# Norms inside their neighbouring stages, tokens in natural order, fewer fences and 1 MB expert pieces in a two-block transformer kernel

## The reference

```python
def first_block(x, ...):
    h = rmsnorm(x, norm_mix_g)
    proj = h @ w_in                        # 1024 x 7424
    # qkv_a: three dilated window attentions (dilations 1, 4, 16), 8 heads each, merged by log-sum-exp
    # q_b, k_b, v_b: dense grouped-query attention, 8 query heads on 2 key heads
    gates = sigmoid(gate_logits + b_gate)
    merged = gates[0] * (o_a @ w_proj_a) + gates[1] * (o_b @ w_proj_b)
    x = x + merged @ w_out
    h2 = rmsnorm(x, norm_ffn_g)
    x = x + moe_ffn(h2, ...)               # router, top 4 of 32 experts, 1024 -> 2 x 1024 -> 1024

def second_block(x, ...):
    for l in range(2):
        proj = rmsnorm(x, pre_g[l]) @ w_in[l]
        y_a = sgu_mixer(...) * silu(z_a)         # gated unit: a 128 x 128 product over tokens
        y_b = mla_mixer(...) * silu(z_b)         # attention over latents
        y_c = chunk_band_mixer(...) * silu(z_c)  # banded attention with a bias table
        merged = sum over 3 branches of sigmoid(gate) * (y @ w_branch)
        x = x + rmsnorm(merged @ w_out[l], post_g[l])
    return x
```

## Time and profile before

| what | value |
|---|---|
| median of three runs | 3405.22 us (3404.34 to 3406.01) |
| the profiled execution | 3412.55 us, its span 3410.7 us |
| TensorE busy (PE) | 3119.5 us, 91% |
| VectorE (DVE), ScalarE (ACT), GpSimd (POOL) busy | 923.4, 751.9, 100.5 us |
| chain that ended last | PE 83%, DMA 6%, DVE 6%, ACT 2% |
| loaded and stored | 575.16 MB, mean 169 GB/s |

### The profile page before, as it was taken

How to read it: one execution, slowest core, us unless ns; L and a number is a source line. 1 busy time by engine, 2 the same in 40 slices (tenths; PEclk the granted TensorE clock), 3 DMA queues, 4 the chain that set the end, 5 groups by cost and what they waited for, 6 DMA issues and landing times.

```text
span 3410.7 us, 36906 instructions
## 1 busy us (share of the span) xinstructions
PE 3119.5 (91%) x13348; PEld 1703.6 (50%) x13349; DVE 923.4 (27%) x2235; ACT 751.9 (22%) x1479; POOL 100.5 (3%) x120
## 2 busy tenths in 40 slices
PE   8999999968999899999899599988999898989997
PEld 4454654445585355574567245444444345444443
DVE  3441651142212222222211323214111224032212
ACT  2222641011212211112211124223111225131111
POOL 0000000000000000000000000010000000010000
PEclk9999999969999999999999798989999999989999
DMA  3221012247989999999994421111221211112221
GB/s 133 74 67 57 1 50 74 87 182 285 414 317 400 411 395 397 416 360 397 423 391 167 173 72 41 37 62 56 75 86 62 80 62 39 57 42 81 80 80 62
DMA packets 110500, 575.16 MB, mean 169 GB/s; under 512 B 13021, under 2 KB 20445, under 8 KB 84672
## 3 DMA queue, kind: packets, MB, share of 16 engines
q1 hardware_dynamic: 100896, 556.76, 42.6%
q0 software_dynamic: 9504, 17.07, 1.3%
HBM read 570.37 MB, written 20.97 MB: 173 GB/s over the span
## 4 chain that ended last, share of the span: by engine, by line
PE 83%; DMA 6%; DVE 6%; ACT 2%; issue 1%; DVEq 1%; ACTq 0%; SPq 0%; POOL 0%; POOLq 0%
PE banks L318 41%; PE banks L1211 12%; PE banks L1189 8%; PE banks L315 6%; PE banks L1164 6%; DMA arena<-in_w_experts 5%; PE banks L600 3%; PE banks L623 2%; PE banks L611 2%; DVE arena L673 1%; PE banks L264 1%; ACT arena L274 1%; DVE arena L685 1%; PE banks L1143 1%; DVE arena L1351 1%
## 5 line engine op out<-in xcount | busy, mean ns | idle before, releaser
L318 PE MATMUL banks<-arena 128*128 128x512 f32 (+3 forms) x3328 | 1419.4, 588 | 36.5 <-DVEq L200 28.1
L318 PEld LDWEIGHTS banks<-arena 128*128 128x128 f32 x3328 | 634.0, 192 | 795.0 <-issue 763.7
L1211 PEld LDWEIGHTS banks<-arena 128*128 128x128 f32 x3584 | 403.3, 193 | 14.5 <-issue 14.5
L1211 PE MATMUL banks<-arena 128*128 128x128 f32 x3584 | 405.0, 276 | 4.7 <-issue 4.7
L1189 PE MATMUL banks<-arena 128*64 128x512 f32 (+1 forms) x1024 | 322.6, 593 | 0.0
L1164 PE MATMUL banks<-arena 128*64 128x512 f32 x1152 | 272.7, 624 | 38.4 <-DMA arena<-in_w_experts 35.8
L315 PE MATMUL banks<-arena 128*128 128x512 f32 x512 | 220.9, 592 | 1.8 <-DVEq L200 1.8
L1189 PEld LDWEIGHTS banks<-arena 128*64 128x64 f32 (+1 forms) x1024 | 123.4, 159 | 176.2 <-issue 176.2
L1284 DVE TENSOR_TENSOR arena<-banks,arena 128x512 f32<-128x512 f32 x64 | 44.3, 692 | 564.1 <-PE banks L1211 321.1
L1164 PEld LDWEIGHTS banks<-arena 128*64 128x64 f32 x1152 | 86.1, 143 | 207.9 <-issue 206.7
L827 DVE TENSOR_TENSOR arena<-banks,arena 128x512 f32<-128x512 f32 x64 | 44.3, 693 | 512.6 <-PE banks L318 512.6
(11 more groups left out here) (208 smaller groups left out, 1822.8 us busy)
## 6 DMA issues: line engine op xcount, KB each, us to landing
arena<-in_w_experts SPq DMA_DIRECT2D x192, 2048.0 KB, 17.8
arena<-in_w_in SPq DMA_DIRECT2D x84, 1024.0 KB, 5.0
arena<-in_w_out SPq DMA_DIRECT2D x12, 1024.0 KB, 5.0
arena<-in_w_branch SPq DMA_DIRECT2D x24, 512.0 KB, 3.6
arena<-expert_rows SPq DMA_DIRECT2D x4, 2048.0 KB, 14.4
arena<-in_w_in SPq DMA_DIRECT2D x4, 832.0 KB, 4.4
arena<-in_gate_b SPq DMA_DIRECT2D x2, 1536.0 KB, 6.2
arena<-in_x SPq DMA_DIRECT2D x4, 512.0 KB, 5.2
```

What stands on the lines that cost most here:

```text
L318: last = PE.matmul(PS[:, tt, 0:ncols], lhsT(kk, tt), Wh[h][:, q, 0:ncols], start=(kk == 0), stop=(kk == kt - 1))
L1211: last = PE.matmul(PS[:, q, f * P:(f + 1) * P], ch[q][:, k, f * P:(f + 1) * P], xT[:, k], start=(k == 0), stop=(k == 7))
```

## The change

- **Norms.** `norm_stage` gives way to a class `Norm` with methods for one tile. `norm_mix` runs as an unfenced stage; `norm_ffn` runs inside `out_stage`, `norm_pre` inside `combine_stage` and inside `out_post_stage` of layer 0. Where the next product begins, PE turns tile by tile ahead of each tile of its first half of K (`turn_ahead`, through a new callable `early`).
- **Order.** x is loaded in residue order by the DMA from an unpermuted input for the first norm, then loaded again in natural order (`x_nat`). The attentions' outputs are written in natural order, POOL reorders `hT` during the dilated attention (`turn_order`), and everything from the output product on is in natural order. The output goes out per tile.
- **Merged turn.** The first half is turned inside the merge's second half, the second half ahead of the tiles of the output product; ACT copies all.
- **Fences.** `norm_mix`, `heads_1`, the output products, `gating`, `latents` and `raised` lose theirs; `raised` loads its weights early and gets its own semaphores; waits (`sgu_seen`, `tr_free`) stand in.
- **Chunk attention.** The bias tiles of the first two head pairs are made during `heads_2`; the gate multiply is split in four.
- **Experts.** Twelve pieces of 1 MB instead of six of 2 MB: each half of gate and up is cut in two by K, and the full-block path accumulates in that order. Ten pieces of expert 0 are loaded after the output product, ahead of the write of the normed rows.

```diff
@@ class Norm
+            def scale(self, dve, c, tt):
+                if tt == 0:
+                    dve.wait_ge(SEM["grow_in"], 16 * c.of("grow") + 16)
+                dve.wait_ge(SEM["norm_sd"], up(c.of("norm_sd") + tt + 1))
+                sd = self.sd[:, tt:tt + 1]
+                V.reciprocal(sd, sd)
+                V.drain()
+                V.scalar_tensor_tensor(self.hb(c)[:, tt], x3[:, tt], sd, v(GROW, D), ALU.mult, ALU.mult).then_inc(SEM["norm_h"], 1)
...
+            def turn_ahead(self, pe, c):
+
+                def early(tt):
+                    if tt == 0:
+                        self.turn(pe, c, 0)
+                    if tt + 1 < TT:
+                        self.turn(pe, c, tt + 1)
+                    pe.wait_ge(SEM["tr_free"], up(c.of("tr") + 2 * tt + 2))
+                return early
@@ heads_1, dilated
+                sp.wait_ge(SEM["norm_h"], up(4))
+                sp.dma_start(x3, A["x"][0].rearrange("(t p) d -> p t d", p=P)).then_inc(SEM["x_nat"], 16)
...
+            def turn_order(pool, c):
+
+                for k in range(0, 8, 2):
+                    for q in range(2):
+                        G.tensor_copy(v(GROW + S * q, S).rearrange("p (u r) -> p r u", r=4),
+                                      hT[:, k + q].rearrange("p (r u) -> p r u", r=4))
+                    G.drain()
+                    G.tensor_copy(hT[:, k:k + 2], v2(GROW, 2, S))
+                    G.drain()
@@ merge_stage, out_products
+            def turn(pe, c0, n, tt):
+                pe.wait_ge(SEM["applied"], up(c0.inside(n, KC).of("sig") + 4 * (nbr - 1) + tt + 1))
+                tr_pe(pe, c0, 4 * n + tt, [merged_3[:, tt, (4 * n + a) * P:(4 * n + a + 1) * P] for a in range(4)])
...
-                        dense_pe(pe, c, 2 * b, lambda kk, tt: yT[b][:, kk, tt * P:(tt + 1) * P], 4, 512)
+                        dense_pe(pe, c, 2 * b, lambda kk, tt: yT[b][:, kk, tt * P:(tt + 1) * P], 4, 512,
+                                 (lambda tt: turn(pe, c0, 0, tt)) if n and not b else None)
...
+                    dense_pe(pe, c0.inside(n, {"T": 1}), 0, lambda kk, tt: mT[:, kk, tt * P:(tt + 1) * P], 8, 512,
+                             None if n else copied, early=None if n else lambda tt: turn_last(pe, c0, tt))
@@ out_stage
+                sp.wait_ge(SEM["mm"], up(unit(c, 1, TT - 1)))
+                for q in range(2, 12):
+                    sp.dma_start(v(BIG + CH * q, CH), A["w_experts"][0, q]).then_inc(SEM[f"ch{q}"], 16)
+                sp.wait_ge(SEM["norm_h"], up(c.of("norm_h") + 4))
+                sp.dma_start(H2D.rearrange("(t p) d -> p t d", p=P), norm_ffn.hb(c)).then_inc(SEM["h2_out"], 16)
...
+                        if n and tt:
+                            norm_ffn.mean(dve, c0, tt - 1)
+                            norm_ffn.scale(dve, c0, tt - 1)
@@ expert_stage
+                    for q in range(12):
+                        sp.wait_ge(SEM["ch_free"], up(12 * j + q + 1))
+                        apart(sp, 12 * j + q + 1)
+                        sp.dma_start(v(BIG + CH * q, CH), A["w_experts"][bass.ds(e, 1), q].rearrange("o p n -> p (o n)")).then_inc(SEM[f"ch{q}"], 16)
...
+                        for h in range(2):
+                            for kh in range(2):
+                                arrived(part(2 * h, 4 * kh))
+                                arrived(part(2 * h + 1, 4 * kh))
+                                if h and kh:
+                                    turn_products(0)
+                                products(h, range(4 * kh, 4 * kh + 4)).then_inc(SEM["ch_free"], 2)
@@ combine_stage
+                    last.then_inc(SEM["x_done"], 1)
+                    if tt:
+                        norm_pre.mean(dve, c, tt - 1)
+                        norm_pre.scale(dve, c, tt - 1)
@@ latents, raised
+                pe.wait_ge(SEM["sgu_seen"], up(c.of("layer") + 1))
...
+                        if n:
+                            pe.wait_ge(SEM["raised_ev"], up(raised_unit(layer, n - 1, tt)))
+                        else:
+                            pe.wait_ge(SEM["ev"], up(unit(c, -1, tt)))
+                            pe.wait_ge(SEM["tr_free"], up(c.of("tr") - 3 + tt))
@@ chunk_stages
-                V.tensor_tensor(v(YC, 2048), v(YC, 2048), v(SC, 2048), ALU.mult)
-            heads = Stage({"T": 4}, sp=sp_, pe=pe_, act=act_, dve=dve_, lead=lead)
+                for q in range(4):
+                    dve.wait_ge(SEM["ev"], up(unit(c, 3, q)))
+                    V.tensor_tensor(v(YC + 512 * q, 512), v(YC + 512 * q, 512), v(SC + 512 * q, 512), ALU.mult)
+            heads = Stage({"T": 4}, sp=sp_, pe=pe_, act=act_, dve=dve_, lead=lead, pool=lambda pool, c: biases(pool, c, (0, 1)))
@@ out_post_stage, ACT
+                        if n:
+                            root(tt)
+                            if tt and more:
+                                norm_pre.square(act, c, tt - 1)
+                                norm_pre.root(act, c, tt - 1)
+                if more:
+                    norm_pre.copy(act, c, 0)
+                    norm_pre.square(act, c, TT - 1)
+                    norm_pre.root(act, c, TT - 1)
+                    for tt in range(1, TT):
+                        norm_pre.copy(act, c, tt)
@@ output_stage
+                for tt in range(TT):
+                    sp.wait_ge(SEM["x_done"], up(8 + tt + 1))
+                    sp.dma_start(out[0, tt * P:(tt + 1) * P], x3[:, tt]).then_inc(SEM["x_out"], 16)
```

464 lines of the change are left out of this document (246 added, 218 removed).

## The result

The changed kernel takes 3312.85 us (median of four runs, 3308.66 to 3317.64) against 3404.78 (3404.18 to 3406.01): a ratio of 0.973 (95% interval 0.971 to 0.975), 91.9 us less. Forecast were 3315 us and -90.3. A second set of five runs of the same kernel gave 3314.17 (3309.81 to 3316.71).

What follows compares the result with a forecast made beforehand. PE, busy 91% of the span, bounds the kernel, so only its waits and slow clock can yield time; terms sum to -90.3 us, execution 3322.3, median 3315 us, range 3296 to 3338.

Steps and rivals of the forecast that it cites:

- Merged turn: Three seams between merge and output product: fences and bunched transposes go, 7.6 us each, -22.9 us in all.
- Gated unit to latents, raised: Two seams, twice each: PE no longer waits for DVE's tail (-20.3 us); raised projections start earlier (-10.4 us).
- Combine, layer seam, output: Combine and norm go tile by tile (-11.6 us), likewise the layer seam (-6.0); output leaves per tile (-2.8).
- Chunk attention: Twice: scores start 1.6 us earlier and DVE's first top stops waiting for POOL, 5.8 us; -14.8 us in all.
- Experts: 1 MB weight pieces: earlier-freed buffers against slower short rows, taken as 0, with ends -18 and +22 us.
- Loss: ... 2% slower: Experts' weight queue: rows cut from 16 KB to 8 KB make transfers 2% slower, by a line through two packet sizes.
- fine pieces win: Rival in the experts: waits fall to about 35 us, giving 3297 us; chance 0.17.
- The walk through the blocks: All 32 expert blocks traced with a first-in first-out queue: -9 us with no rate loss, +3 at 2%.
- slower than before: Rival in the experts: 1 MB pieces don't overlap their fixed part, 62 us an expert, 4150 us; chance 0.03.
- POOL in the dilated attention: POOL's reordering of `hT` stays hidden in the 86 us stage, its overlap inside DVE's idle time; cost 0.
- POOL's instructions block DVE whole: Rival in the dilated attention: 12 POOL instructions of up to 3.5 us hold DVE, +10 us, 3325; chance 0.05.
- Norm and router: Seam behind the first output product: norm per tile, bound by a DVE and ACT chain, saves only 1.0 us.

Runs made afterwards that it cites:

- e4: Changed kernel with one fence put back ahead of the latents' products, twice in the run: median 3333.87 us.
- f1: Changed kernel with four repairs: earlier first turns, POOL's copies tied to scores, combine loads reordered, ACT's tile 0 copy earlier at the layer seam: 3309.31 us.
- e6: Changed kernel with the first two head pairs' bias tiles made inside chunk attention again and the gate multiply in one instruction: 3326.20 us.
- e2: Changed kernel with experts' weights waited for and freed by 2 MB again, each piece sent as two 1 MB transfers with 8 KB rows: 3320.45 us.
- f2: f1 plus idle matmuls that nobody reads in three PE pauses (ahead of the router, layer seam, combine): 3301.00 us.
- f3: f1 with all combine rows loaded ahead of the next weights, and idle matmuls ahead of the router only: 3308.77 us.
- f4: f3 with idle matmuls at the layer seam and during the combine as well: 3301.84 us.
- e7: Changed kernel with the last half of the merged tiles turned in one go ahead of the output product, no fence back: 3326.36 us.
- e1: Changed kernel with the experts' weights in six 2 MB pieces and the expert loop of before: 3317.81 us.

## Why the prediction was right, and where its terms were not

- **Merged turn.** Forecast 7.6 a seam, measured 7.7, 9.6, 7.8; most of the extra of the second is the clock of the kernel before (its merge products took 249.13 us there and 247.44 in the third). The eight turns take 0.43 us each with no pause.
- **Gated unit to latents, raised.** Forecast 15.4 a layer, measured 15.3 and 15.0; e4 measured the fence alone at 10.7, forecast 10.3 and 10.0.
- **Combine, layer seam, output.** -13.1, -5.9, -3.8 for -11.6, -6.0, -2.8. The order that sets the seam, ACT's copy of tile 0 behind its root of tile 2, is there (product at 2600.27, idle 2.69 behind ACT L280), and moving it (f1) gave 3.2 more. The forecast's "about 11 us of idle PE" for this seam does not fit its own -6.0: PE stood 13.0 us there before and 7.5 now.
- **Chunk attention.** The idle time was right (7.1 of 7.4 in e6); what I left out is the clock behind the pause, 2.9 us in e6's first layer. The whole stretch got 10.1 and 8.0 us shorter for 7.4.
- **Experts: the term that failed, inside its ends.** The step "Loss: ... 2% slower" took the slower queue to cost about as much as the finer freeing gains. The rate did fall by 2%, but in e2 that cost 0.5 us, within the spread of the stage, while the freeing gained 12 of the 25 us that I had called its most. So the rival "fine pieces win" had the mechanism and over half of its size; 0.17 was too low for it. Why the lower rate cost so little stays open: the changed kernel's queue moved over 410 GB/s in about half of the stage, which isn't little. The walk through the blocks with no loss of rate gave -9, which is nearer to the -11 than the 0 that I took.
- **The rival "slower than before".** It did not come. The price of 2.0 us plus bytes/436e3 that I quoted from the Trainium skill, "DMA: Bandwidth & Descriptors", stands there in the section "Anatomy of one DMA — SWDGE (gpsimd) path" and not in "Bandwidth", and for transfers that GpSimd issues; here SP issues them. The section "Bandwidth" asks for at least 1 MiB a transfer, which 1 MB pieces still meet. In the changed kernel an expert took 1083.5/31 = 35 us and not the 53 of that rule one transfer at a time.
- **POOL in the dilated attention.** The forecast took 0 and gave "POOL's instructions block DVE whole" a chance of 0.05. It happened: 4 to 6 us, and its sign, a DVE instruction of over 1 us (1.81), showed in the trace. The failed step took 0.62 against 0.49 us as the price of any overlap. Those 0.62 us lay wholly inside an instruction of POOL:

```profile
2295.04 0.93 POOL L1673 TENSOR_SCALAR arena<-arena 128x256 f32<-128x256 f32 x1
```

The scale began 0.06 us behind it and ended 0.25 us ahead of its end, so the reading was right for POOL's TENSOR_SCALAR. It did not carry over to POOL's COPY, which held DVE to its end; in the changed kernel both stand in one trace (a 512-wide scale of 0.62 us beside a TENSOR_SCALAR at 2962.45). Why the two differ, no run here shows. The copies were quicker than I thought (1.1 us for 512 columns, 13 us in all, not 28 to 69), which kept the loss under the rival's 10. The Trainium skill, "SBUF — State Buffer", section "SBUF: two separate sides", says that the ports which DVE and GpSimd share go for a whole instruction to whichever starts first, GpSimd's instruction or one of DVE that runs in a 2-port mode or has two inputs in SBUF. Beside POOL's copies the trace agrees in the main, with ends of both within 0.03 us, and DVE's L696 with an operand from PSUM was not held; beside POOL's TENSOR_SCALAR it does not.
- **Norm and router.** The seam itself got 2.2 us shorter, more than the 1.0; behind it the router's 64 products took 13.87 us, 10.12 before. Nine further traces with that code show 13.86 or 13.87 in eight and 11.24 in one. Before, 32 transposes ran in one go ahead of them; now PE turns in short groups between pauses, and the clock is at 0.50 when the router starts. f2 shows that it is the clock, since with PE kept busy the products took 11.35, and 10.72 and 10.83 in f3 and f4. The forecast ended this term at the router's first product.
- **Start.** I had the first product begin 0.5 us earlier; it began at 20.71, 0.1 later than before. And I left out that the turns of the last two tiles, which used to lie ahead of the product, now stand inside it at 0.87 us each: +1.9 in all.

The median came out 2 us from the forecast, and that is luck. Stage by stage the traced difference is 13 us more than forecast: experts -11.6, chunk, merge, combine and output -8.0 and latent attention -3.2 beyond it, against dilated +4.2, start +2.4 and router +3.1. The medians differ by 92 us and not by 103 because the traced execution of the kernel before lay 8 us above its median and that of the changed one 4 below. That a sum is right is no proof of its terms.

## What to carry to other kernels

Price a seam as pause plus the clock behind it: here 7.5 us of standing cost 10.7, and a shorter, choppier seam ahead of small matmuls gave its gain back. When loads run through few buffers, ask at what size a buffer comes free before asking for the best transfer; halving 2 MB pieces paid, halving again lost. Before moving copies to POOL, look at which DVE instructions work on SBUF alone meanwhile, and tie each copy to a DVE instruction that reads PSUM; take the price of an overlap only from a row with the same instruction on POOL.

## What the runs showed of the hardware beyond that

- PE's clock can fall while PE hardly stands: in f2 it was granted 1.00 over 6.2 us of wide matmuls and 0.70 over the transposes and 32-column products behind them, in which PE is busy 13.26 of 14.20 us with one pause of 0.88. The fall came in the midst of the 32-column products, while PE was busy throughout:

```profile
701.79:704.60 2.81, 2.81 (x25) 2.81 (x26) 0.00 (x0) 0.00 (x0) 0.00 (x0) 0.99 1.01 417
704.60:713.14 8.54, 8.54 (x41) 8.40 (x40) 0.00 (x0) 0.00 (x0) 0.00 (x0) 0.50 1.01 414
```

  In the changed kernel, with pauses of 0.79 and 3.21 us ahead, the clock was at 0.50 over the transposes and all 64 products.
- The same code takes a different time from execution to execution where PE stands often and shortly: over the thirteen traces of the changed kernel and its variants the latent attention with the first two chunk products took 106.5 to 114.1 us, while merge and output product of a layer took 305.88 or 305.89 in all but e7. The length goes with the granted clock of the stretch, 0.98 at 106.5 us and 0.91 at 114.1. How much of the spread of 3 to 12 us between runs of one kernel this makes stays open: of the 4.8 us between the two traces of the changed kernel it is 1.6.
- Between the medians of two kernels that spread hides a few us: e1's lies only 4 to 5 us over the changed kernel's, where its stage is 11 longer. For terms of this size the stage in the trace decides.
